# Recurrence gates as pairs of 64-row products, and a new order on VectorE and ScalarE

## The reference

```python
xb = xf.reshape(bsz, t, LRU_HEADS, LRU_BLOCK)          # 8 heads of 64 channels
r = sigmoid(einsum('bthi,hij->bthj', xb, w_a) + b_a)
i = sigmoid(einsum('bthi,hij->bthj', xb, w_x) + b_x)
log_a = -LRU_C * r * softplus(-lam)
a = exp(log_a)
gated_x = sqrt(-expm1(2.0 * log_a)) * (i * xf)
h = scan(h <- a * h + gated_x)
y_a = h * silu(g_a)
```

## Time and profile before

| | |
|---|---|
| median of 3 runs | 1351.75 us (1351.18 to 1354.14) |
| profiled execution, its own time | 1351.93 us |
| its span, first to last instruction | 1349.7 us |
| TensorE busy | 1320.4 us (98%) |
| VectorE, ScalarE, GpSimd busy | 856.4, 434.6, 331.1 us |
| granted TensorE clock, mean | 0.999 |

### The profile page before, as it was taken

One profiled execution on the slowest core, in us unless ns is written; L12 is line 12 of the kernel. 1 busy time (PEld: TensorE's weight loads), 2 busy tenths in 40 slices (PEclk: granted clock), 3 DMA queues, 4 the chain that ended last, 5 costly groups with the idle time before them and its releaser, 6 DMA issues.

```text
span 1349.7 us, 27665 instructions
## 1 busy us (share of the span) xinstructions
PE 1320.4 (98%) x11328; PEld 900.3 (67%) x11328; DVE 856.4 (63%) x1939; ACT 434.6 (32%) x1044; POOL 331.1 (25%) x450
## 2 busy tenths in 40 slices
PE   5999999999999999999999999999999999999998
PEld 3577776666653454567877778877888778875543
DVE  4747874455444475684886858858588685882246
ACT  4213443344431232521423314233142241422221
POOL 1023200010014132523322323123231242212352
PEclk9999999999999999999999999999999999999999
DMA  9521007002036332211112112121121211441124
GB/s 370 236 63 36 13 28 279 1 1 79 3 131 211 152 115 78 38 56 36 64 35 69 34 44 89 35 69 35 34 89 44 69 35 34 138 148 26 34 96 169
DMA packets 63298, 111.98 MB, mean 83 GB/s; under 512 B 34778, under 2 KB 38690, under 8 KB 61618
## 3 DMA queue, kind: packets, MB, share of 16 engines
q1 hardware_dynamic: 63172, 110.21, 24.3%
HBM read 91.79 MB, written 18.40 MB: 82 GB/s over the span
## 4 chain that ended last, share of the span: by engine, by line
PE 86%; DVE 7%; DMA 3%; POOL 1%; issue 1%; ACT 1%; SPq 0%; DVEq 0%; POOLq 0%; ACTq 0%
PE psum L1132 82%; PE psum L1135 4%; DMA mem<-modw 2%; DVE mem L2965 1%; DVE mem L2776 1%; DVE mem L3290 1%; DMA mem<-x_dram 1%; DVE mem L3056 0%; DMA y<-mem 0%; DVE mem L3167 0%; DVE mem L2945 0%; POOL mem L954 0%; DVE mem L2782 0%; ACT mem L2089 0%; DVE mem L3044 0%
## 5 line engine op out<-in xcount | busy, mean ns | idle before, releaser
L1132 PE MATMUL psum<-mem 32*32 32x32 f32 (+11 forms) x10720 | 1258.4, 304 | 6.3 <-DVE mem L2477 1.5
L1132 PEld LDWEIGHTS psum<-mem 32*32 32x32 f32 (+3 forms) x10720 | 832.1, 142 | 401.2 <-issue 215.6
L2965 DVE SCALAR_TENSOR_TENSOR mem<-mem 128x576 f32<-128x576 f32 (+1 forms) x126 | 106.4, 845 | 0.0
L1135 PE MATMUL psum<-mem 128*128 128x128 f32 (+1 forms) x608 | 85.3, 278 | 16.3 <-ACT mem L1929 12.4
L1135 PEld LDWEIGHTS psum<-mem 128*128 128x128 f32 (+1 forms) x608 | 70.7, 144 | 40.7 <-issue 20.2
L2280 ACT ACTIVATE mem<-mem 128x128 f32<-128x128 f32 x72 | 22.0, 305 | 127.6 <-DVE mem L3215 74.4
L2166 ACT ACTIVATE mem<-psum 128x288 f32<-128x288 f32 x28 | 11.4, 407 | 104.0 <-PE psum L1132 104.0
L1011 POOL COPY mem<-mem 128x3 f32<-128x3 f32 x24 | 8.3, 348 | 148.9 <-DVE mem L2923 70.7
L2058 ACT ACTIVATE mem<-mem 128x256 f32<-128x256 f32 x72 | 35.5, 495 | 24.8 <-DVE mem L2699 24.8
L2746 DVE TENSOR_TENSOR mem<-mem,psum 128x512 f32<-128x512 f32 x28 | 19.2, 685 | 37.3 <-PE psum L1132 36.9
L2176 ACT ACTIVATE mem<-mem 128x576 f32<-128x576 f32 (+1 forms) x42 | 32.7, 780 | 28.0 <-DVE mem L2943 28.0
(11 more groups left out here) (260 smaller groups left out, 1278.3 us busy)
## 6 DMA issues: line engine op xcount, KB each, us to landing
mem<-modw SPq DMA_DIRECT2D x12, 2048.0 KB, 11.8
mem<-w SPq DMA_DIRECT2D x44, 512.0 KB, 4.3
mem<-x SPq DMA_DIRECT2D x10, 512.0 KB, 4.7
x_dram<-mem SPq DMA_DIRECT2D x9, 512.0 KB, 2.9
mem<-row_dram SPq DMA_DIRECT2D x8, 576.0 KB, 5.1
mem<-x_dram SPq DMA_DIRECT2D x9, 512.0 KB, 3.7
mem<-wout SPq DMA_DIRECT2D x1, 4096.0 KB, 15.0
mem<-gs SPq DMA_DIRECT2D x8, 512.0 KB, 3.6
```

The source lines that it names most:

```text
L1132: return pe.matmul(*a, **k)
L1135: return pe.transpose(out, in_, ident[0:n, 0:n])
L2965: x = dve.scalar_tensor_tensor(cvm, U1[:, m, lo + j:hi + j], CW[:, 3 * g + ORDER[m], j:j + 1], cvm, ALU.mult, ALU.add)
```

## The change

The gates of a third are now two products of 64 rows, `gw[r]` for partitions 0 to 63 and 64 to 127, each with 128 columns of weights: 64 for gate a and 64 for gate x. The lower half goes to bank 6 and the upper half to bank 7. `gw` shrinks to 2 x 64 columns, is loaded in three pieces, and for the upper half stands with the gates exchanged. ScalarE empties each part with four Tanh of 64 partitions. Parts 1 and 2 no longer follow part 0 at once. They stand behind the two pieces of step "1" of the pair, or, for m = 3, before the second and third projection. On VectorE the chain is split (`chain`, `recur`, `recur_samples`), and its pieces, the sums and the gates stand in a new order. The c21 gates and the product by `lh` move into the next round, ahead of its chain, and `lh` shares memory with `lg` in place of `ti`.

```diff
-        gw = take(2, P)
+        gw = take(2, HD)
-        lh = ti
+        lh = lg
@@ SyncE
-                    sp.wait_ge(sem("l_mm"), 6 * m)
-                sp.dma_start(gw, I["gw"][m]).then_inc(sem("gw_in"), 16)
+                    sp.wait_ge(sem("l_mm"), 3 * m)
+                lo, hi = slice(0, HD), slice(HD, P)
+                sp.dma_start(gw[lo], I["gw"][m, lo, :, lo]).then_inc(sem("gw_in"), 16)
+                for i in range(2):
+                    sp.dma_start(gw[hi, i], I["gw"][m, hi, 1 - i, hi]).then_inc(sem("gw_in"), 16)
@@ TensorE, pair(p, between) and gates(m)
                     part("1", j, w1, 0, HT, 0, lo(j))
+                    between(j)
...
-                for i in range(6):
...
+                def part(n):
+                    if m or n:
+                        pe.wait_ge(sem("lz_ev"), 12 * m + 4 * n)
+                    for q in range(2):
+                        r = slice(q * HD, q * HD + HD)
+                        i = mm(B(6 + q)[:, 0:NC], gw[r].rearrange("p g c -> p (g c)"),
+                               xc[r, n * NC:(n + 1) * NC], start=True, stop=True)
+                    i.then_inc(sem("l_mm"), 1)
+                part(0)
                 if m < LM - 1:
-                    pair(m + 1)
+                    pair(m + 1, lambda j: part(j + 1))
                     return
...
+                    if q == 0 and n:
+                        part(n)
@@ ScalarE, lru(m)
-                for i in range(6):
...
+                if m:
+                    wait(act, sem("l_a"), m)
+                    wait(act, sem("l_w"), 2 * m)
+                for n in range(3):
+                    if m and n == 1:
+                        gate_tanh(m - 1, "c21", U3c)
+                    wait(act, sem("l_mm"), 3 * m + n + 1)
+                    for i, dst in enumerate((tr, ti)):
+                        for q in range(2):
+                            r, s = (slice(x * HD, x * HD + HD) for x in (q, q ^ i))
+                            act.activation(dst[r, n * NC:(n + 1) * NC], B(6 + q)[s, 0:NC], ACT.Tanh, scale=0.5,
+                                           bias=gbias[r, m, i:i + 1]).then_inc(sem("lz_ev"), 1)
...
-                for name, src in (("c11", P1c), ("c22", V22), ("c21", U3c)):
+                for name, src in (("c11", P1c), ("c22", V22)):
@@ VectorE, lru(m); chain(m) now ends before the root is awaited
+                if m:
+                    gates(m - 1, "c21", U3c)
...
+                    dve.scalar_tensor_tensor(YT[:, m - 1], lh, 0.5, YT[:, m - 1], ALU.mult, ALU.mult
+                                             ).then_inc(sem("l_y"), 1)
                 chain(m)
+                if m:
+                    gates(m - 1, "c12", U2c)
...
+                added(p, "u2")
                 added(p, "c11")
                 conv0(m + 1, 0)
                 added(p, "u3")
-                conv0(m + 1, 1)
-                gates(m, "c11", P1c)
+                recur(m)
                 added(p, "c22")
                 added(p, "u4")
+                conv0(m + 1, 1)
+                added(p, "c21")
+                recur_samples(m)
+                gates(m, "c11", P1c)
                 gates(m, "c22", V22)
-                added(p, "c21")
-                gates(m, "c21", U3c)
...
                 added(p, "c12")
```

More of the change, by code:

```diff
@@ L1240, in project, with pair @@
                     i.then_inc(sem(sname), 1)
-            def pair(p):
+            def pair(p, between=lambda j: None):
                 w1, w2 = PAIR_W[p]
@@ L1294, in gates, with last_free @@
                     pe.wait_ge(sem("mod_done"), 1)
-                for i in range(6):
[L1296 to L1299, removed]
+                def part(n):
[7 more added lines that the diff above has]
+                part(0)
                 if m < LM - 1:
-                    pair(m + 1)
+                    pair(m + 1, lambda j: part(j + 1))
                     return
+                def last_free(q, n):
+                    if q == 0 and n:
+                        part(n)
+                    pe.wait_ge(sem("st_add"), STEPS * (PAIRS - 1) + LAST_FREE[3 * q + n])
                 for q in range(2):
                     pe.wait_ge(sem(f"w0_in{q}"), 16 * m + 48)
-                    project(m, q, "g_mm", lambda n: pe.wait_ge(
-                        sem("st_add"), STEPS * (PAIRS - 1) + LAST_FREE[3 * q + n]))
+                    project(m, q, "g_mm", lambda n: last_free(q, n))
             tiles(LM, gates)
@@ L1988, in lru @@
                     wait(act, sem("dve_step"), DVE_STEP["l_const"])
-                for i in range(6):
[L1990 to L1998, removed]
+                if m:
[10 more added lines that the diff above has]
+                                           bias=gbias[r, m, i:i + 1]).then_inc(sem("lz_ev"), 1)
+                wait(act, sem("lz_ev"), 12 * m + 10)
                 c.mark(act.activation(la, tr, ACT.Exp, scale=ksp[:, m:m + 1], bias=ksp[:, m:m + 1]))
@@ L2006, in lru @@
                     gate_tanh(m - 1, "c12", U2c)
-                wait(act, sem("l_w"), m + 1)
+                wait(act, sem("l_w"), 2 * m + 1)
                 act.activation(lw_, lw_, ACT.Sqrt).then_inc(sem("l_sq"), 1)
@@ L2567, in conv0 @@
                 if m:
-                    dve.wait_ge(sem("l_mm"), 6 * m)
+                    dve.wait_ge(sem("l_mm"), 3 * m)
                     c.sync()
@@ L2605, in chain, with recur @@
                 c.mark(dve.scalar_tensor_tensor(ti, ti, 1.0, xc, ALU.add, ALU.mult))
[L2606 to L2609, removed]
+            def recur(m):
                 dve.wait_ge(sem("l_sq"), m + 1)
                 c.sync()
-                c.mark(dve.scalar_tensor_tensor(lg, ti, 0.5, lw_, ALU.mult, ALU.mult))
+                c.tell(dve.scalar_tensor_tensor(lg, ti, 0.5, lw_, ALU.mult, ALU.mult), sem("l_w"), 2 * m + 2)
                 c.sync()
@@ L2615, in chain, with recur_samples @@
                                               ALU.mult, ALU.add))
+            def recur_samples(m):
                 for s in range(NS):
@@ L2624, in lru @@
             def lru(m):
+                if m:
+                    gates(m - 1, "c21", U3c)
+                    dve.wait_ge(sem("g_ev"), G_PAIR * (m - 1) + OUTS["c21"] + 2)
+                    dve.scalar_tensor_tensor(YT[:, m - 1], lh, 0.5, YT[:, m - 1], ALU.mult, ALU.mult
+                                             ).then_inc(sem("l_y"), 1)
+                    dve.wait_ge(sem("l_y"), m)
                 chain(m)
+                if m:
+                    gates(m - 1, "c12", U2c)
                 if m == LM - 1:
+                    recur(m)
+                    recur_samples(m)
                     for g in range(6):
@@ L2642, in lru @@
                 added(p, "u3")
-                conv0(m + 1, 1)
-                gates(m, "c11", P1c)
+                recur(m)
                 added(p, "c22")
                 added(p, "u4")
+                conv0(m + 1, 1)
+                added(p, "c21")
+                recur_samples(m)
+                gates(m, "c11", P1c)
                 gates(m, "c22", V22)
-                added(p, "c21")
-                gates(m, "c21", U3c)
-                dve.wait_ge(sem("g_ev"), G_PAIR * m + OUTS["c21"] + 2)
-                dve.scalar_tensor_tensor(YT[:, m], lh, 0.5, YT[:, m], ALU.mult, ALU.mult
-                                         ).then_inc(sem("l_y"), 1)
                 added(p, "c12")
```

6 lines of the change are left out of this document (3 added, 3 removed).

## The result

The changed kernel takes 1365.93 us (median of four runs, 1364.38 to 1366.57), the kernel before, on the same chip, 1352.54 (1351.18 to 1354.14). The ratio is 1.0097, with a 95% interval of 1.0079 to 1.0114: 13.4 us slower. The forecast was 1355.0, in a range of 1349.0 to 1360.5. The direction was right, the size was not, and the result lies outside the range.

A forecast was written before the change was run, and what follows sets the result against it. TensorE, busy 1320.4 of 1349.7 us, was taken to bound the kernel; after the change a ScalarE-VectorE ring with GpSimd contention would bind. Projections ending at 236.5 instead of 233.4 gave 1351.93 + 3.2 - 0.2 = 1355.0 us, range 1349.0 to 1360.5.

The forecast's parts named there:

- The part on TensorE: Two 64-row gate products side by side: 1.06 us a part, twelve 12.7 instead of 17.9; TensorE alone would gain 5.2.
- rival D: Clearly slower: halves not side by side (part 1.70 us, 1360.8), or half Tanh not overlapping (0.58 pitch, 1360); chance 0.17.
- Half the partitions save nothing: ScalarE's gate Tanh: 64 partitions take as long as 128, by rows of 592 against 598 ns for 512 columns.
- The pitch in a row is 0.48: ScalarE's gate Tanh in a row start 0.48 us apart, so a part's four take 2.02 us.
- the ring's first stretch: From the first Tanh of part 0, through three parts, Exp and Tanh, to VectorE's chain: 10.7 us.
- TensorE's wait at part 1: TensorE waits nearly 3 us for part 0's four Tanh, at m = 1 and m = 2.
- The ring through the c11 gates and c22 Tanh: First Tanh of m wait behind c22 Tanh, which need half-buffers freed by VectorE's late c11 gates: 31.3 us a round before contention.
- The ring's two sums: First Tanh to VectorE's chain, 10.7 us, and from there to the next first Tanh, 20.6 us before contention.
- Contention: GpSimd's weight sums slow VectorE's recurrence: 2.2 us a round, plus 0.7 for the fourth sum in the first round.
- rival B: Not slower: the scan slips past GpSimd or the sums fall beside PSUM adds; 1350 to 1352.2 us, chance 0.24.
- c12 late at the first projection: First projection needs c12, which VectorE adds after the c22 gates, at 203.4: TensorE waits 1.9 us.
- The sum: Projections end at 236.5 instead of 233.4, +3.1, say +3.2; 1351.93 + 3.2 - 0.2 = 1355.0 us.

The follow-up runs named there:

- the rebuilt kernel: Changed kernel with four Tanh a part, each of 128 partitions, half the gates' values in wrong halves: 1360.51 us; with ten idle products ahead of TensorE's waits also, 1355.86.
- the four quarters: Changed kernel with gates as four products of 64 rows and 64 columns, one bank emptied whole, c11 gates and c12 add early: 1350.98 us, ratio 0.9996 to the kernel before.

## Why the prediction was wrong, step by step

- **The part on TensorE: right.** Forecast 1.06 us, side by side. In the change, and in the run with both banks emptied whole, a part takes 1.04 us at full clock, counted from the pass before it to the second pass behind it, less two passes. The first half of rival D (1.70) fell.
- **"Half the partitions save nothing": right.** 575 ns for 64 partitions, 580 for 128.
- **"The pitch in a row is 0.48": wrong, the first step that failed.** It was read off a 128-partition Tanh and used for 64. Measured 0.60; four take 2.38 us and not 2.02, and the ring's first stretch, from the first Tanh to the chain, 11.8 and not 10.7. The earlier trace rows looked like cover for it, but they show the duration of one, not what the next may overlap. The second half of rival D had this case, with 0.58 and 1360 us, at a chance that it shared with the halves. Giving ScalarE the forecast pitch, in the changed kernel with half of the gates' values in the wrong halves, took 1365.9 to 1360.5, so 5.4 us (4.6 with the clock held), some of it because a shorter wait let the clock stay up at m = 1.
- **TensorE's wait at part 1 counted at its own length: wrong, the second step.** I forecast waits of almost 3 us there and about 2 at the projection, and priced the passes behind them at 0.242 and 0.322. They ran at 1.2 GHz (0.480 and 0.640) after waits of 3.35, 2.5 and 2.8 us. No rival had it. Holding the clock gave 5.5 us in the change and 4.6 (1360.5 to 1355.9) once the pitch was right. No row before the change showed such a stretch, since its clock was 0.999; but a forecast that makes TensorE wait for 3 us has to ask the question. It is a risk and not a fixed price: waits of 2.83 us without GpSimd's sums and of 2.56 us at m = 1 with 128-partition Tanh left the clock full. One wait also sat elsewhere than forecast: at m = 2 TensorE waited 2.5 us at part 0 for xc and 1.0 at part 1, where I had nearly 3 at part 1. The Trainium skill, "TensorE: Matmul & The Clock Gate" (HAM oscillation — how this bites in real kernels), warns that a wait between bursts can send the engine back to the low clock; the trace of the change agrees, by the three waits above.
- **The ring through the c11 gates and c22 Tanh: right.** Moving the gates gave 7.9 us in the change. The ring's two sums were right to 0.3 us in each round, as the rebuilt kernel shows: 10.5 to 10.6 us from the first Tanh to the chain (forecast 10.7), and from there to the next first Tanh 22.4, 22.8 and 20.9 (forecast 22.7, 22.8 and 20.8 with contention where it was expected).
- **Contention: right in kind and place.** Forecast 2.9 and 2.2 us in the two rounds, measured 2.3 and 3.2 with narrow Tanh. The scan is held up by GpSimd (3.24 against 2.29), which decides against rival B.
- **c12 late at the first projection: right in place.** Forecast 1.9, measured 2.8. wqkv, as forecast, costs nothing.
- **The sum.** 1355.0 forecast, 0.9 of rest, 4.6 of clock and 5.4 of pitch give the measured 1365.9. The terms are differences of measured times, so they must close; what is shown is that 0.9 is small. Taken in the other order the clock is 5.5 and the pitch 4.6.

One piece stays open. In the profiled run of the change TensorE's clock also fell at 26 us, far ahead of anything that the change touches, which cost about 1.2 us. It did so in the profiled runs of four other versions as well (64 rows with the c11 gates moved, 128 rows with the c12 add early, the four quarters, and the 128-partition Tanh with the clock left alone), and not in that of the kernel before or of the other ten. The change and its version with idle products execute the same up to there, and only one shows it, which speaks against a hand of the change in it. It was not tried by itself. Also open is why a narrow Tanh lets nothing overlap.

## What to carry to other kernels

With 384 columns an eviction of fewer than 128 partitions costs ScalarE more than a full one (0.60 against 0.48 us), so cutting a product into halves that have to be emptied one by one can give back on ScalarE several times what TensorE gains: 0.25 us a part here against 1.3. And a forecast wait of TensorE is not only its own length: look at the granted clock of what follows it, which can be half or full behind waits of the same length, above all where the slowed passes feed the ring that made the wait. Where an interleaved order is forecast to wait anyway, take its waits away first (here one move of the c11 gates, 7.9 us, a part of it clock).

## What the runs showed of the hardware that I had not expected

- On ScalarE, with 384 columns from PSUM and a bias operand: pitch 0.48 us at 128 partitions, 0.60 at 96, 64 and 32. Without the bias 0.39 and 0.51.
- Ten products whose results nobody reads, put in at three places where TensorE waits or has just waited, made the kernel 5.5 us faster.
- Behind waits of 2.83 us TensorE's clock fell to 1.2 GHz in one kernel and stayed full in another.
- Four products of 64 rows and 64 columns on the four quarters, two passes each, take 1.01 us with the change of shape, no more than two of 64 rows and 128 columns (1.04).
- A scan on VectorE beside GpSimd's sums went from 2.29 to 3.24 us, the first of the short sample scans from about 0.2 to 1.2.
